# Prompt attention by pairs of heads side by side, each pair's output taken out first in VectorE's step

## The chip, the cores and the metric

One core of one Trainium2 chip. The metric is the device time of one execution of the whole kernel, in microseconds (us); the median of three runs of the kernel before is 2034.86 us (2034.53 to 2036.19).

## What is computed

One layer of a hybrid decoder, for a prompt of 1024 tokens and for 64 sample tokens: a token mixer (latent attention beside a depthwise convolution), cross attention to a memory, a gated feed-forward part. The change touches only the prompt's latent attention, 8 heads over 1024 positions with a causal mask:

```python
s = (jnp.einsum('bqhl,btl->bhqt', ql, c_keys) + jnp.einsum('bqhr,btr->bhqt', qp, pe_keys)) * ATTN_SCALE
s = jnp.where(pos[:, None] >= k_pos[None, :], s, NEG_INF)
pr = jax.nn.softmax(s, axis=-1)
o_lat = jnp.einsum('bhqt,btl->bqhl', pr, c_keys)
attn = jnp.einsum('bshl,lhv->bshv', o_lat, p['w_uv'])
```

The kernel forms keys (64 + 32 features per head) and values (64 per head) from the latents first, and multiplies `pr` by the values.

## The kernel before

The kernel is one program of stages, each with its own semaphores and with the instructions of every engine written out in order. `prompt_attention_stage` (L700) is the one in question. Its data are feature-major: `K.x[:, pair, token]` holds the attention output of heads 2·pair (partitions 0 to 63) and 2·pair+1 (64 to 127).

The work is cut into 64 **tiles** n = 8h + i: head h, block i of 128 queries. By causality block i sees keys 0 to 128(i+1)-1, so a tile of i = 7 has eight times the work of one of i = 0. For each tile:

- `scores(n)` on TensorE (L848): queries times keys into two of PSUM's banks (0, 1 or 2, 3 in turn).
- `find_top(n)` on VectorE (L1010, L1012, L1014): mask on the diagonal block, the row maximum, its negative.
- `exp(n)` on ScalarE (L941): probabilities into `prob[n % 2]`.
- `turn_tile(n)` on TensorE (L868): i+1 transposes of 128x128 into banks 4 and 5 (`turn`).
- `copy_turned(n)` on ScalarE (L949): to `prob_t[n % 2]`.
- `attend(n)` on TensorE (L878): i+1 products of turned probabilities (stationary, 128 columns) and `K.v[:, j, h, :]` (moving, 65 columns: 64 values and a column of ones, whose product is the row's sum). The result `o_acc` in bank 6 has a query per partition.
- `take_out(n)` on VectorE (L1020, L1024): the reciprocal of the sum, and the product with it into `o`.

An f32 matmul is two instructions in the profile, a transpose one. When a pair of heads is done, `o` of four blocks is transposed by `turn_pair` (L855) in two of the next pair's steps, and `copy_pair` (L955) puts it in `K.x`. Beside the tiles run the **jobs** that make queries (`q`, L826, three k-steps of 512 columns) and keys (`k`, L830, two); each has one accumulator bank and is read by ScalarE (L929, L932) and, for `q`, by three VectorE instructions of the rotary part (L999, L1000, L1003, `rope_job`). Four jobs stand at the start (`AT_START`), the others in steps i = 0, 1, 2 of each head. At given steps VectorE also does a part of the convolution's layer norm (`NORM_AT`, L1032, L1035), and ScalarE ends the stage with four Silu (L987).

The order is fixed by these loops; on TensorE:

```python
for n in range(TILES):
    turn_tile(n)
    if n + 2 < TILES:
        scores(n + 2)
    for what, which, half in jobs_beside(*divmod(n, QT)):
        job(what, which, half)
    if n >= 1:
        attend(n - 1)
```

VectorE's step n is `find_top(n + 2)`, `take_out(n - 1)`, the rotary part of the job. `attend(n)` waits until `take_out(n - 1)` has emptied `o_acc` (semaphore `o_out`).

## Time and profile before

| | |
|---|---|
| median of 3 runs | 2034.86 us (2034.53 to 2036.19) |
| the profiled execution | 2033.87 us, span 2032.0 us, mean granted clock 0.970 |
| TensorE matmul, of the span | 1857.1 us (91%) |
| VectorE, ScalarE, GpSimd | 1174.8, 481.8, 589.3 us |
| prompt attention, first to last tile's turn | 436.5 to 658.8 us |
| in it, busy: TensorE, VectorE, ScalarE | 209.8, 142.6, 100.9 of 222.3 us |

Times within the profile are from the start of the span. PE is TensorE's matmuls, PEld its weight loads (which overlap the matmuls), DVE is VectorE, ACT ScalarE. A matmul's duration contains its way through the array, which the next one overlaps; what one of a row of matmuls costs is the distance from start to start. In a merged row of N instructions it is (length - duration of one) / (N - 1). In forms such as `128*64 128x256` the first pair is rows*columns of the stationary operand, the second the moving operand.

### The profile page before, as it was taken

The page shows a single profiled execution, that of the slowest core. Times are in us where ns is not written, and L with a number is a line of the kernel's source. Part 1 is how long each engine was busy: PE and PEld are TensorE (multiplying, and loading weights), DVE is VectorE, ACT ScalarE, POOL GpSimd, SP SyncE. Part 2 cuts the span into 40 slices and gives each one's busy share as a digit, 9 for nine tenths or more (in the row PEclk, how much of TensorE's full clock was granted, in tenths as well). Part 3 has the DMA queues.
Part 4 walks back from the last instruction along what each step waited for, and adds up shares of the span by engine and source line. Part 5 has one row for each costly group of instructions (what it writes and reads, how often), then busy time and mean ns, then how long its engine had stood idle before and what let it go on. Part 6 is the DMA issues. An engine that isn't in the chain of part 4 may idle for free. (4 is left out here: it accounts for less than half of the span.)

```text
span 2032.0 us, 27594 instructions
## 1 busy us (share of the span) xinstructions
PE 1857.1 (91%) x10840; PEld 1657.8 (82%) x10840; DVE 1174.8 (58%) x1665; ACT 481.8 (24%) x810; POOL 589.3 (29%) x437
## 2 busy tenths in 40 slices
PE   6998888699999899899859989999999999999995
PEld 6998554356667898788729879999999999999983
DVE  7886599866665337333323797445454554545547
ACT  4021332144444423222222341001100100110011
POOL 3331489710000124321013722223222322232220
PEclk9999899799999999999989989999999999999997
DMA  5214422100000214400451211111111111111102
GB/s 160 99 42 58 173 94 94 32 31 1 1 1 1 85 48 156 144 21 10 164 213 52 94 42 42 42 41 41 51 42 41 41 51 42 41 41 49 44 14 88
DMA packets 42715, 128.42 MB, mean 63 GB/s; under 512 B 12464, under 2 KB 18736, under 8 KB 40016
## 3 DMA queue, kind: packets, MB, share of 16 engines
q1 hardware_dynamic: 39984, 105.17, 15.7%
q0 software_dynamic: 1792, 18.88, 2.4%
q10 hardware_dynamic: 864, 3.34, 0.5%
q8 instruction: 52, 0.85, 0.2%
q14 instruction: 23, 0.19, 0.0%
HBM read 118.81 MB, written 8.56 MB: 63 GB/s over the span
## 5 line engine op out<-in xcount | busy, mean ns | idle before, releaser
L252 POOL CAST w_hi<-raw 128x1024 fp32r<-128x1024 f32 x90 | 98.0, 1088 | 811.3 <-issue 319.7
L281 PE MATMUL ps<-xo_hi,w_hi 128*128 128x384 f32 (+1 forms) x1248 | 292.5, 332 | 18.3 <-DVE xo_lo L2644 6.2
L281 PE MATMUL ps<-xo_lo,w_hi 128*128 128x384 f32 (+1 forms) x1248 | 290.5, 331 | 0.0
L281 PE MATMUL ps<-xo_hi,w_lo 128*128 128x384 f32 (+1 forms) x1248 | 289.9, 330 | 0.0
L281 PEld LDWEIGHTS ps<-xo_hi,w_hi 128*128 128x128 f32 x1248 | 218.1, 189 | 22.2 <-issue 13.2
L254 POOL TENSOR_TENSOR w_lo<-raw,w_hi 128x1024 fp32r<-128x1024 f32 x90 | 221.1, 2456 | 7.2
L281 PEld LDWEIGHTS ps<-xo_lo,w_hi 128*128 128x128 f32 x1248 | 218.7, 190 | 0.2
L281 PEld LDWEIGHTS ps<-xo_hi,w_lo 128*128 128x128 f32 x1248 | 218.3, 189 | 0.0
L2597 DVE TENSOR_TENSOR xo<-ps,xo 128x768 f32<-128x768 f32 (+1 forms) x160 | 108.4, 719 | 130.6 <-PE ps L281 130.6
L377 DVE SCALAR_TENSOR_TENSOR x<-u_prompt,vecs,x 128x1024 f32<-128x1024 f32 x120 | 164.7, 1373 | 3.4
L2549 DVE TENSOR_TENSOR ffn_g_prompt<-ffn_g_prompt,ffn_rstd 128x1024 f32<-128x1024 f32 x22 | 67.4, 3062 | 167.2 <-ACT ffn_g_sample L2414 167.2
L281 PE MATMUL ps<-ffn_hid_hi,w_hi 128*128 128x384 f32 (+2 forms) x528 | 128.4, 342 | 4.8 <-DVE ffn_hid_lo L2586 4.8
L281 PE MATMUL ps<-ffn_hid_lo,w_hi 128*128 128x384 f32 (+2 forms) x528 | 123.6, 332 | 0.0
L281 PE MATMUL ps<-ffn_hid_hi,w_lo 128*128 128x384 f32 (+2 forms) x528 | 121.8, 329 | 0.0
L281 PE MATMUL ps<-hx_hi,w_hi 128*128 128x384 f32 (+1 forms) x384 | 90.9, 346 | 11.9 <-PEq L1475 5.4
L1540 POOL CAST w_hi<-raw 128x1024 fp32r<-128x1024 f32 x8 | 8.3, 1036 | 313.9 <-PE ps L281 283.1
L281 PEld LDWEIGHTS ps<-ffn_hid_hi,w_hi 128*128 128x128 f32 x528 | 91.1, 190 | 8.4 <-DVE ffn_hid_lo L2586 5.1
L878 PEld LDWEIGHTS ps<-v,mla_prob_t 128*128 128x128 f32 x576 | 72.8, 192 | 27.7 <-issue 23.4
L281 PEld LDWEIGHTS ps<-ffn_hid_lo,w_hi 128*128 128x128 f32 x528 | 91.9, 190 | 3.3 <-issue 3.0
L2423 ACT ACTIVATE ffn_hid_hi<-ffn_hid 128x1088 fp32r<-128x1088 f32 x22 | 24.5, 1114 | 289.5 <-PE ps L281 253.6
L281 PE MATMUL ps<-h_hi,w_hi 128*128 128x384 f32 x336 | 77.2, 338 | 16.7 <-POOL w_lo L473 11.7
L281 PEld LDWEIGHTS ps<-ffn_hid_hi,w_lo 128*128 128x128 f32 x528 | 91.6, 190 | 0.6
(348 smaller groups left out, 3352.6 us busy)
## 6 DMA issues: line engine op xcount, KB each, us to landing
raw<-in_units SPq DMA_DIRECT2D x128, 512.0 KB, 3.3
xs_keys<-in_cache_k_t SPq DMA_DIRECT2D x8, 1024.0 KB, 8.3
xs_vals<-in_cache_v_t SPq DMA_DIRECT2D x16, 512.0 KB, 13.3
x<-in_x_t SPq DMA_DIRECT2D x8, 544.0 KB, 9.3
out_y_t<-x SPq DMA_DIRECT2D x2, 1792.0 KB, 6.6
out_old<-in_x_t ACTq DMA_DIRECT2D x6, 544.0 KB, 4.0
mla_wq<-in_w_q_t SPq DMA_DIRECT2D x1, 1536.0 KB, 8.3
out_kv_latent_t<-c SPq DMA_DIRECT2D x1, 1088.0 KB, 13.0
```

Source lines behind the costliest of these rows:

```text
L252: nc.gpsimd.tensor_copy(K.w_hi[:, s, :], K.raw[:, s, :]).then_inc(K.hi_done[s], 1)
L254: nc.gpsimd.tensor_tensor(K.w_lo[:, s, :], K.raw[:, s, :], K.w_hi[:, s, :].bitcast(F32), ALU.subtract).then_inc(K.split_done[s], 1)
L281: mm = nc.tensor.matmul(out(at, n), w, x(k, at, n), start=first and k == 0 and p == 0, stop=last and k == len(tiles) - 1 and p == 2)
L377: ops.scalar_tensor_tensor(cv, u, scale, cv, ALU.mult, ALU.add).then_inc(tapped, 1)
L878: mm = nc.tensor.matmul(o_acc, prob_t[:, n % 2 * QT + j, :], K.v[:, j, h, :], start=j == 0, stop=j == i)
L1540: nc.gpsimd.tensor_copy(K.w_hi[:, s, :], K.raw[:, s, :]).then_inc(K.hi_done[s], 1)
L2423: nc.scalar.activation(hid_hi[:, slot, :], hid[:, :], ACT.Identity).then_inc(hid_hi_made, 1)
L2549: nc.vector.tensor_tensor(g_p, g_p, rstd[:, 0:SEQ], ALU.mult).then_inc(g_scaled, 1)
L2597: ins = nc.vector.tensor_tensor(y_at, acc, y_at, ALU.add)
```

## The change

Tiles are ordered by **rounds** of 16: `place(n)` takes the two heads of a pair in turn, block by block (tile 2m is head 2p, tile 2m+1 head 2p+1, same block i = m % 8). What was done per tile behind the turned copy is now done per pair m of tiles (32 pairs):

- `attend(m)`: the values are the stationary operand (64 columns) and the turned probabilities the moving one (128 columns). Head 2p's product goes to partitions 0 to 63 of `o_acc`, head 2p+1's to 64 to 127, the two in turn for each j. The result is feature-major.
- The sums come from `exp` (`accum_out` into `den`). `make_diagonals(m)` on VectorE takes the reciprocal (128x2) and makes two diagonal matrices of 128x128 from the identity; two f32 matmuls of ones and diagonal spread the inverses over partitions as `row_acc` (bank 6 too).
- `take_out(m)` on VectorE copies `row_acc` to `inv_row` and multiplies `o_acc` by it into `K.x`; it stands ahead of `find_top` in every odd step from 3. `o`, `turn_pair`, `copy_pair` and the column of ones are gone.
- `prob_t` has four buffers, `qh` four; the next pair's jobs (four q, two k) stand in steps r = 0 to 5 of a round, and `AT_START` has six jobs, of which three come behind the first two scores.

```diff
+        AT_START = [("q", 0, 0), ("k", 0, 0), ("q", 1, 0), ("q", 0, 1), ("k", 0, 1), ("q", 1, 1)]
+        FIRST_JOBS = 3
+        def place(n):
+            p, r = divmod(n, ROUND)
+            return 2 * p + r % 2, r // 2
+        def jobs_beside(n):
+            p, r = divmod(n, ROUND)
+            if p + 1 == HEADS // 2 or r >= 6:
+                return []
+            return [[("q", 2 * p + 2, 0), ("k", p + 1, 0), ("q", 2 * p + 3, 0), ("q", 2 * p + 2, 1), ("k", p + 1, 1),
+                     ("q", 2 * p + 3, 1)][r]]
...
+        o_acc, row_acc = K.ps[:, 6, 0:P], K.ps[:, 6, P:2 * P]
+        def half(h):
+            return slice(h % 2 * VH, (h % 2 + 1) * VH)
...
-            def attend(n):
-                h, i = divmod(n, QT)
-                pe.wait_ge(turned_copied, n + 1)
-                if n >= 1:
-                    pe.wait_ge(o_out, n)
+            def attend(m):
+                i = m % QT
+                pe.wait_ge(turned_copied, 2 * m + 2)
+                if m >= 1:
+                    pe.wait_ge(out, m)
                 for j in range(i + 1):
-                    mm = nc.tensor.matmul(o_acc, prob_t[:, n % 2 * QT + j, :], K.v[:, j, h, :], start=j == 0,
-                                          stop=j == i)
-                mm.then_inc(attended, 1)
+                    for n in (2 * m, 2 * m + 1):
+                        h = place(n)[0]
+                        nc.tensor.matmul(o_acc[half(h)], K.v[:, j, h, 0:VH], prob_t[:, n % 4 * QT + j, :], start=j == 0,
+                                         stop=j == i)
+                pe.wait_ge(diagonal_made, 2 * m + 2)
+                for par in range(2):
+                    nc.tensor.matmul(row_acc[half(par)], K.ones[:, 0:VH], diagonal[:, m % 2, par, :], start=True,
+                                     stop=True).then_inc(attended, 1)
...
+            for job_of in AT_START[:FIRST_JOBS]:
+                job(*job_of)
             scores(0)
             scores(1)
+            for job_of in AT_START[FIRST_JOBS:]:
+                job(*job_of)
...
-                if n >= 1:
-                    attend(n - 1)
+                if n % 2 == 0 and n >= 2:
+                    attend(n // 2 - 1)
...
-                nc.scalar.activation(prob[:, n % 2, 0:(i + 1) * P], score(n), ACT.Exp, bias=neg_top[:, i:i + 1],
-                                     scale=SCALE).then_inc(exped, 1)
+                nc.scalar.activation(prob[:, n % 2, 0:(i + 1) * P], score(n), ACT.Exp, bias=neg_top[:, r:r + 1],
+                                     scale=SCALE, accum_out=den[:, r:r + 1]).then_inc(exped, 1)
...
-            def take_out(n):
-                h, i = divmod(n, QT)
-                dve.wait_ge(attended, n + 1)
-                nc.vector.reciprocal(inv[:, i:i + 1], o_acc[:, VH:]).then_inc(inv_ready, 1)
-                dve.wait_ge(inv_ready, n + 1)
-                if h >= 2:
-                    dve.wait_ge(o_turned, 2 * (h // 2 - 1) + i // 4 + 1)
-                nc.vector.tensor_scalar(o[:, i, h % 2 * VH:(h % 2 + 1) * VH], o_acc[:, 0:VH], inv[:, i:i + 1], None,
-                                        ALU.mult).then_inc(o_out, 1)
+            def make_diagonals(m):
+                r = 2 * (m % QT)
+                dve.wait_ge(exped, 2 * m + 2)
+                nc.vector.reciprocal(inv[:, r:r + 2], den[:, r:r + 2]).then_inc(inv_ready, 1)
+                dve.wait_ge(inv_ready, m + 1)
+                for par in range(2):
+                    nc.vector.tensor_scalar(diagonal[:, m % 2, par, :], K.ident[:, :], inv[:, r + par:r + par + 1], None,
+                                            ALU.mult).then_inc(diagonal_made, 1)
+            def take_out(m):
+                p, i = divmod(m, QT)
+                dve.wait_ge(attended, 2 * m + 2)
+                if m >= 1:
+                    dve.wait_ge(out, m)
+                nc.vector.tensor_copy(inv_row[:, :], row_acc).then_inc(row_out, 1)
+                dve.wait_ge(row_out, m + 1)
+                nc.vector.tensor_tensor(K.x[:, p, i * P:(i + 1) * P], o_acc, inv_row[:, :], ALU.mult).then_inc(out, 1)
...
             for n in range(TILES):
+                if n % 2 == 1 and n >= 3:
+                    take_out(n // 2 - 1)
                 if n + 2 < TILES:
                     find_top(n + 2)
-                if n >= 1:
-                    take_out(n - 1)
-                for what, which, half in jobs_beside(*divmod(n, QT)):
+                if n % 2 == 1:
+                    make_diagonals(n // 2)
+                for what, which, half_of in jobs_beside(n):
                     if what == "q":
-                        rope_job(which, half)
+                        rope_job(which, half_of)
```

TensorE in the middle of a head, of before: every step has its turn (L868), scores (L848) and attend (L878).

```order
L878 MATMUL ps<-v,mla_prob_t 128x65 [waits mla_o_out,mla_turned_copied]
L878 MATMUL ps<-v,mla_prob_t 128x65 x3
L868 MATMUL ps<-ident,mla_prob 128x128 [waits mla_turned_copied,mla_exped]
L868 MATMUL ps<-ident,mla_prob 128x128 x5
L848 MATMUL ps<-mla_kh,mla_qh 128x512 [waits mla_exped]
L848 MATMUL ps<-mla_kh,mla_qh 128x512
L878 MATMUL ps<-v,mla_prob_t 128x65 [waits mla_o_out,mla_turned_copied]
L878 MATMUL ps<-v,mla_prob_t 128x65 x4
```

Here an attend stands between any two turns.

The same place of the change; 64x128 is the output's shape.

```order
L858 MATMUL ps<-ident,mla_prob 128x128 [waits mla_turned_copied,mla_exped]
L858 MATMUL ps<-ident,mla_prob 128x128 x4
L849 MATMUL ps<-mla_kh,mla_qh 128x512 [waits mla_exped]
L849 MATMUL ps<-mla_kh,mla_qh 128x256
L858 MATMUL ps<-ident,mla_prob 128x128 [waits mla_turned_copied,mla_exped]
L858 MATMUL ps<-ident,mla_prob 128x128 x5
L849 MATMUL ps<-mla_kh,mla_qh 128x512 [waits mla_exped]
L849 MATMUL ps<-mla_kh,mla_qh 128x384
L871 MATMUL ps<-mla_prob_t,v 64x128 [waits mla_out,mla_turned_copied]
L871 MATMUL ps<-mla_prob_t,v 64x128 x9
L875 MATMUL ps<-mla_diagonal,ones 64x128 [waits mla_diagonal_made]
L875 MATMUL ps<-mla_diagonal,ones 64x128
```

Two steps of turn and scores now stand between two attends, and each attend ends with two more matmuls that wait for VectorE's diagonals.

VectorE in the middle of a round, of the change:

```order
L1018 COPY mla_inv_row<-ps 128x128 [waits mla_out,mla_attended]
L1020 TENSOR_TENSOR x<-ps,mla_inv_row 128x128 [waits mla_row_out]
L997 TENSOR_TENSOR ps<-ps,causal 128x128 [waits mla_scored]
L999 TENSOR_REDUCE mla_top<-ps 128x1 [waits mla_masked]
L1001 TENSOR_SCALAR mla_neg_top<-mla_top 128x1 [waits mla_top_found]
L1007 RECIPROCAL mla_inv<-mla_den 128x2 [waits mla_exped]
L1010 TENSOR_SCALAR mla_diagonal<-ident,mla_inv 128x128 [waits mla_inv_ready]
L1010 TENSOR_SCALAR mla_diagonal<-ident,mla_inv 128x128
L997 TENSOR_TENSOR ps<-ps,causal 128x128 [waits mla_scored]
L999 TENSOR_REDUCE mla_top<-ps 128x1 [waits mla_masked]
L1001 TENSOR_SCALAR mla_neg_top<-mla_top 128x1 [waits mla_top_found]
```

An odd step has five instructions more than an even one; before, each step had its three of the maximum and two of taking out.

## Rows read from the trace of the kernel before

**Rows 1.** Stretches: us; busy (x instructions) PE, PEld, DVE, ACT, POOL; clock; DMA.
```profile
436.50:658.80 222.30, 209.79 (x1157) 147.20 (x1157) 142.61 (x366) 100.93 (x159) 0.00 (x0) 1.00 0.00 1
```

**Rows 2.** Groups of instructions, 436.5 to 658.8, costliest first.
```profile
L878 PE MATMUL ps<-v,mla_prob_t 128*128 128x65 f32 x549 | 69.5, 271 | 5.6 <-DVE mla_o L1024 5.6
L868 PE MATMUL ps<-ident,mla_prob 128*128 128x128 f32 x288 | 42.6, 275 | 3.1 <-ACT mla_prob L941 2.4
```

**Rows 3.** Who waited for whom, 436.5 to 658.8: total us, times, longest.
```profile
DVE ps L1010 <- PE ps L848: 26.5, 27, 2.0
PE ps L878 <- DVE mla_o L1024: 5.6, 17, 0.7
PE ps L830 <- DVE mla_part L1000: 5.6, 6, 1.0
```

**Rows 4.** TensorE's matmuls in order of time: start us, length, merged count, idle before.
```profile
580.47 1.06 PE L868 MATMUL ps<-ident,mla_prob 128*128 128x128 f32 x8
...
581.81 1.67 PE L878 MATMUL ps<-v,mla_prob_t 128*128 128x65 f32 x14
```

**Rows 5.** The same view: a query job of the stage, then the paged stage.
```profile
621.32 2.74 PE L826 MATMUL ps<-qn,mla_wq 128*128 128x512 f32 x6
...
376.56 1.89 PE L1246 MATMUL ps<-v,paged_q_lat 128*64 128x512 f32 x8
...
239.15 1.95 PE L1281 MATMUL ps<-x,paged_prob_t 128*64 128x256 f32 x16
```

**Rows 6.** The same view: the paged stage where the stationary operand's form changes.
```profile
230.14 0.40 PE L1254 MATMUL ps<-c,paged_q_lat 128*64 128x64 f32 x4
230.47 0.66 PE L1231 MATMUL ps<-ident,past_rope 128*128 128x128 f32 x4
...
373.09 1.89 PE L1246 MATMUL ps<-v,paged_q_lat 128*64 128x512 f32 x8
375.09 0.63 PE L1290 MATMUL ps<-paged_fold,paged_o 128*128 128x64 f32 x4
```

**Rows 7.** VectorE's groups of the whole span, shapes apart.
```profile
L1010 DVE TENSOR_TENSOR ps<-ps,causal 128x128 f32<-128x128 f32 x64 | 19.0, 296 | 27.0 <-PE ps L848 26.5
L1024 DVE TENSOR_SCALAR mla_o<-ps,mla_inv 128x64 f32<-128x64 f32 x64 | 18.2, 284 | 2.3
L1020 DVE RECIPROCAL mla_inv<-ps 128x1 f32<-128x1 f32 x64 | 10.4, 163 | 47.2 <-PE ps L878 47.0
L1012 DVE TENSOR_REDUCE mla_top<-ps 128x1 f32<-128x640 f32 x8 | 6.6, 824 | 0.3
...
L1012 DVE TENSOR_REDUCE mla_top<-ps 128x1 f32<-128x256 f32 x8 | 3.4, 425 | 0.3
L1982 DVE COPY xq_sample<-xp_q 128x128 f32 x3 | 0.7, 227 | 0.4
L1389 DVE TENSOR_TENSOR paged_fold<-ident 128x64 f32<-128x64 f32 x1 | 0.2, 160 | 0.0
```

**Rows 8.** ScalarE in order of time, and one of its groups (cross attention's exp).
```profile
581.57 1.02 ACT L949 ACTIVATE mla_prob_t<-ps 128x1024 f32<-128x1024 f32 x1 [0.99 <-PE ps L868]
...
L1915 ACT ACTIVATION_READ_ACCUMULATOR xp_prob<-ps,xp_neg_top 128x1 f32 x32 | 6.2, 192 | 0.0
```

**Rows 9.** The stage's start, engines mixed, in order of time.
```profile
433.24 0.68 DVE L1003 TENSOR_TENSOR mla_qh<-mla_part 32x512 f32<-32x512 f32 x1
...
436.55 0.30 PE L868 MATMUL ps<-ident,mla_prob 128*128 128x128 f32 x1 [2.40 <-ACT mla_prob L941]
```

**Rows 10.** The stage's end, engines mixed, in order of time.
```profile
658.78 1.02 ACT L949 ACTIVATE mla_prob_t<-ps 128x1024 f32<-128x1024 f32 x1 [1.25 <-PE ps L868]
...
660.92 1.97 PE L878 MATMUL ps<-v,mla_prob_t 128*128 128x65 f32 x16 [0.67 <-DVE mla_o L1024]
661.12 4.48 ACT L987 ACTIVATE x<-x,vecs 128x1088 f32<-128x1088 f32 x4
...
665.50 1.05 ACT L955 ACTIVATE x<-ps 128x512 f32<-128x512 f32 x2
```

More of the change, by code:

```diff
@@ L730, in prompt_attention_stage @@
         wq, wuk = sb("wq", [P, HEADS, KQ * P]), sb("wuk", [P, HEADS // 2, KC * P])
-        qh = [sb(f"qh{s}", [P, SEQ]) for s in range(2)]
+        qh = [sb(f"qh{s}", [P, SEQ]) for s in range(4)]
         kh = [K.kh] + [sb(f"kh{s}", [P, SEQ]) for s in range(1, 4)]
@@ L790, in _ @@
         def _(pool):
-            nc.gpsimd.memset(K.v[:, :, :, VH:], 1.0).then_inc(ones_set, 1)
             split_units(nc, pool, K, 1)
@@ L847, in scores @@
                     w = min(512, (i + 1) * P - at)
-                    mm = nc.tensor.matmul(score(n)[:, at:at + w], qh[h % 2][0:96, i * P:(i + 1) * P],
+                    mm = nc.tensor.matmul(score(n)[:, at:at + w], qh[h % 4][0:96, i * P:(i + 1) * P],
                                           key_buffer(h)[0:96, at:at + w], start=True, stop=True)
                 mm.then_inc(scored, 1)
-            def turn_pair(pair, half, to):
-                pe.wait_ge(o_out, (2 * pair + 1) * QT + 4 * half + 4)
-                for j in range(4):
-                    mm = nc.tensor.transpose(to[:, j * P:(j + 1) * P], o[:, 4 * half + j, :], K.ident[:, :])
-                return mm
             def turn_tile(n):
@@ L861, in turn_tile @@
                     pe.wait_ge(turned_copied, n)
-                    if pair_beside(n - 1) is not None:
-                        pair, half = pair_beside(n - 1)
-                        pe.wait_ge(out, 2 * pair + half + 1)
-                if pair_beside(n) is not None:
-                    turn_pair(*pair_beside(n), turned_pair(n)).then_inc(o_turned, 1)
-                for j in range(n % QT + 1):
+                for j in range(place(n)[1] + 1):
                     mm = nc.tensor.transpose(turn[:, j * P:(j + 1) * P], prob[:, n % 2, j * P:(j + 1) * P],
@@ L890, in _ @@
             pe.wait_ge(w_in, 32)
-            for what, which, half in AT_START:
-                job(what, which, half)
+            for job_of in AT_START[:FIRST_JOBS]:
+                job(*job_of)
             scores(0)
             scores(1)
+            for job_of in AT_START[FIRST_JOBS:]:
+                job(*job_of)
             pe.wait_ge(rooted, 2)
-            pe.wait_ge(ones_set, 1)
             for n in range(TILES):
@@ L901, in _ @@
                     scores(n + 2)
-                for what, which, half in jobs_beside(*divmod(n, QT)):
-                    job(what, which, half)
-                if n >= 1:
-                    attend(n - 1)
-            attend(TILES - 1)
-            pe.wait_ge(turned_copied, TILES)
-            for half in range(2):
-                turn_pair(HEADS // 2 - 1, half, turn[:, half * 512:(half + 1) * 512]).then_inc(o_turned, 1)
+                for job_of in jobs_beside(n):
+                    job(*job_of)
+                if n % 2 == 0 and n >= 2:
+                    attend(n // 2 - 1)
+            attend(TILES // 2 - 1)
         @block.scalar
@@ L971, in _ @@
                                      ).then_inc(rooted, 1)
-            for what, which, half in AT_START:
-                copy_job(what, which, half)
+            for job_of in AT_START[:FIRST_JOBS]:
+                copy_job(*job_of)
             exp(0)
             exp(1)
+            for job_of in AT_START[FIRST_JOBS:]:
+                copy_job(*job_of)
             for n in range(TILES):
                 copy_turned(n)
-                if pair_beside(n) is not None:
-                    copy_pair(*pair_beside(n), turned_pair(n))
                 if n + 2 < TILES:
                     exp(n + 2)
-                for what, which, half in jobs_beside(*divmod(n, QT)):
-                    copy_job(what, which, half)
+                for job_of in jobs_beside(n):
+                    copy_job(*job_of)
             for k in range(KU):
@@ L987, in _ @@
                 nc.scalar.activation(cv[k], cv[k], ACT.Silu, bias=vec(K, "b_cln", k)).then_inc(acted, 1)
-            for half in range(2):
-                copy_pair(HEADS // 2 - 1, half, turn[:, half * 512:(half + 1) * 512])
         @block.vector
@@ L1064, in _ @@
             for n in range(TILES):
+                if n % 2 == 1 and n >= 3:
+                    take_out(n // 2 - 1)
                 if n + 2 < TILES:
                     find_top(n + 2)
-                if n >= 1:
-                    take_out(n - 1)
-                for what, which, half in jobs_beside(*divmod(n, QT)):
+                if n % 2 == 1:
+                    make_diagonals(n // 2)
+                for what, which, half_of in jobs_beside(n):
                     if what == "q":
-                        rope_job(which, half)
+                        rope_job(which, half_of)
                 if n in NORM_AT:
```

66 lines of the change are left out of this document (25 added, 41 removed).

## Prediction

> **What bounds the kernel now.** I first read the stretches [rows 1]. From the first tile's turn (436.5) to the last one's (658.8) TensorE's matmuls are busy for 209.8 of 222.3 us at the full granted clock (1.00, the level of 2.4 GHz); VectorE has 142.6, ScalarE 100.9. So this stretch runs at TensorE's pace with short holes, and a change is worth what it takes from TensorE there. The groups [rows 2] show where it goes: the value products of L878 are the costliest, 69.5 us.
>
> What one instruction costs is read from start to start [rows 4]. Fourteen of L878 last 1.67 us: (1.67 - 0.27)/13 = 0.108 us each; with the start of a group 0.109. The transposes of L868 cost (1.06 - 0.275)/7 = 0.112. The moving operand of L878 is half as wide (65 against 128 columns) and yet it takes as long: what sets it is the stationary operand, 128 columns in both.
>
> The waits [rows 3] show the holes: 17 times L878 waits for VectorE to empty the accumulator (5.6 us), 6 times a key job for the rotary part (5.6 us). The end of the stage [rows 10] is ScalarE's: last turned copy from 658.78, four Silu from 661.12 to 665.6, then two more copies in 1.05 us; TensorE's last two attends lie under the Silu.
>
> **The value products.** 288 f32 products are 576 instructions before and after. What changes is the form: 64 stationary, 128 moving columns, the halves of the output in turn. The trace has this pattern in the paged stage [rows 5]. A 512-column instruction alone costs (2.74 - 0.59)/5 = 0.43 us. Eight of L1246, whose outputs alternate between partitions 0 to 63 and 64 to 127, last 1.89 us, which is four starts 0.43 apart: two run at once. Sixteen of L1281 with 256 columns last 1.95 us: (1.95 - 0.38)/7 = 0.224 per two, 0.112 each, where half of 0.43, 0.215, would be the price alone. So halves overlap, and 128 columns would go at 0.054 each. The other floor is the stationary load of 64 columns: L1254, with 64 moving columns that would need only 0.027, has (0.40 - 0.22)/3 = 0.060 [rows 6]. I take 0.060, the larger; the ends are 0.054 and, without overlap, 0.107.
>
> Up to the last turn 546 of 576 instructions lie before the change (tiles 62 and 63 come behind it), and 544 after it (pair 31 comes behind): 546 x 0.109 = 59.5, 544 x 0.060 = 32.6, together **-26.9 us**.
>
> **Inverses.** 31 pairs x 4 instructions of the same form (64 stationary, 128 moving): 124 x 0.060 = **+7.4**.
>
> **Changing the form.** TensorE now goes from 128 stationary columns to 64 and back in each of 31 pairs. Where the trace does this [rows 6], the last of L1254 starts at 230.14 + 0.40 - 0.22 = 230.32 and the first of L1231 at 230.47: 0.15 instead of 0.06, or 0.09 more. After L1246 the last pair starts at 374.39, streams until 374.82, and L1290 starts at 375.09: 0.27 (a wait for VectorE may be in it). I take 0.10, the nearer case, since nothing else is waited for there: 62 x 0.10 = **+6.2**; ends 0 and +16.7. The Trainium skill, "TensorEngine Tiling (Array Packing)", section Tiling Modes, says that changing the tiling mode, not just the tile, drains TensorE. A drain as long as what of a 0.27 us matmul remains behind its stream (0.16) would make this term +9.9; the rows lie on both sides of that.
>
> **Removed work and waits on TensorE.** 24 of the 32 pair transposes were in the loop: 24 x 0.109 = **-2.6**. The accumulator wait goes: 5.6 us of idle, and in each of the 17 cases the previous matmul's way through the array that stood bare (0.27 - 0.11 = 0.16): **-8.4**. Now `attend(m)` has two steps' turns and scores behind `attend(m-1)`, and `take_out(m-1)` has been put ahead of the maximum in VectorE's step, so it runs while TensorE does these.
>
> **New waits on TensorE.** In an odd step nothing stands between `scores` and the next turn. In the middle of a round the scores cover the copy (two instructions of 0.43 per 512 columns, so 0.214 a block and 1.7 for eight). At a round's end they do not: the turn of tile 16k waits for the copy of eight blocks, 0.2 + 1.02 us [rows 8], over scores of 0.2 us; before, `attend` of 14 instructions stood there (1.67 us, [rows 4]). Three such places, 1.0 each: **+3.0**. `attend` also ends in a wait for the diagonals, which follow `find_top` of the next tile; behind this wait stand the next turn and scores. From block 4 on I find that VectorE needs 0.30 + 0.82 + 0.15 [rows 7] (a negative costs about what a reciprocal of one column does) for the maximum and about 1.0 for the diagonals, against the turn, scores and attend (0.45 + 1.07 + 0.96) that TensorE has in between: just covered, 0.
>
> **The start.** Four jobs become six. The third, a query job, ends as before, and its rotary part at 433.9 [rows 9], then scores; the other three jobs start at 434.3. They wait for each other's readers (one bank): 2.6, then 1.6 of wait, 1.7, 1.5 of wait, 2.6 us: the first turn comes at about 444.3 instead of 436.55, +7.7. Two query jobs (2 x 6 x 0.429 = 5.1 us) leave the loop for it, and the 2.40 us hole before the first turn is filled by them: **+2.6**. The waits among jobs in the loop (5.6 us before) I leave as they are: 0. Five neighbouring pairs of jobs per round can wait, but behind an even step attend covers it, and in the first round there is little to cover with.
>
> **The last pair of heads** has no jobs. VectorE's load per pair of tiles: copy and multiply 0.28 + 0.30 (a copy of that size between SBUF tensors is 0.227, the mask's addition in PSUM 0.296; I put the copy out of PSUM between them), reciprocal 0.16, two diagonals. For these the nearest rows [rows 7] are 0.284 for 64 columns out of PSUM and 0.160 for 64 columns in SBUF; with 64 columns more at 0.07 that is 0.35 or 0.23, and I take 0.35. Together 1.45, with gaps 1.55, against 0.97 before. Two maxima of 256 columns are 2 x (0.30 + 0.43 + 0.15 + 0.10) = 1.95. So VectorE needs 3.5 us for block 1 of a pair and TensorE about 2.2. Blocks 0 to 2 together lose about 4 us, of which the old last head had about 1.5: **+2.5**.
>
> **ScalarE** gets a reading of the accumulator behind each exp, 64 x 0.192 = 12.3 us [rows 8], and loses eight copies of 0.5. It has 100.9 us of 222.3: covered, 0 (at a chain's bare places 0.19 each, inside the roundings above). VectorE gets 32 x 0.58 = 19 us: 162 of some 205; covered in the mean. GpSimd's memset goes: nothing waits for it.
>
> **The end.** From the last turn on ScalarE sets it: the two copies go, **-1.05**. TensorE's last attend (32 x 0.060 + 0.24) and VectorE's 0.6 lie under the Silu. TensorE then idles some 1 us longer before the next stage; I leave what follows from that at 0.
>
> **Sum:** -26.9 + 7.4 + 6.2 - 2.6 - 8.4 + 3.0 + 2.6 + 2.5 - 1.1 = **-17.3 us**. Against the profiled execution's 2033.87 that is 2016.6; the median of the runs is 1.0 above that execution, so 2017.5.
>
> **Rivals.**
> 1. *The halves do not overlap at 128 columns* (a load of one half keeps the other half's matmul from starting), so each costs 0.107: 544 x 0.047 + 124 x 0.047 = +31.4, or 2049, slower than before. The change is slower from 0.060 + 17.3/668 = 0.086 us each. For it: no row has this with 128 moving columns. Against: L1281 reaches its stream's pace with the same alternation. Chance 0.04.
> 2. *VectorE becomes the bound* also where there are jobs. In steps 0 to 5 of a round it has about 6.6 us of maxima, 8.4 of rotary parts, 4.7 for the pairs and up to 2.7 of layer norm or copies, some 20 to 22, against TensorE's 23. If its order costs another 1 us per four pairs it is +8: 2025.5. The Trainium skill, "TensorEngine Tiling (Array Packing)", section PSUM Bottleneck, says that tiling speeds up TensorE but not the emptying of PSUM, which may then bound. For it: VectorE's 162 of 205. Against: 26.5 us of its idle time before a maximum [rows 3] are waits for scores. Chance 0.15.
> 3. *The change of form is dear*, 0.27 each: +10.5, or 2028. Chance 0.08.
> 4. *It goes better*: 0.054 each (-4), no cost of form (-6): 2008. Chance 0.05.
>
> **How the numbers follow.** The forecast has 0.68, with a range of its own of +-5. From 2007 to 2028 the forecast and rivals 2 to 4 lie mostly inside; rival 1 and joint misses stay out. What differs by over 0.2% (4.1 us) can be told from no change. Faster: the forecast, 2 to 4 nearly whole, 0.88. Slower: rival 1 and a joint case of 2 and 3 with a further wait, 0.07. Same: 0.05.
>
> **What would show it.** Attends of 4(i+1) matmuls lasting 0.06 x count + 0.2 (32 in 2.1 us); no wait of the first for VectorE; first turn near 444, last near 642; the inverse's matmuls directly behind; a wait of about 1 us at the turn after a round's end. Wrong would be: starts of attend 0.1 us apart, TensorE waiting for `mla_diagonal` in most pairs, or maxima that VectorE starts without waiting for scores.

## The result, and the profile after

| | before | after |
|---|---|---|
| median of the runs of this comparison | 2037.86 us (2034.53 to 2039.43, 8) | 2028.18 us (2025.59 to 2035.19, 8) |
| ratio to the runs of before | | 0.996, interval 0.9949 to 0.9972 |
| profiled execution, its span | 2033.87, 2032.0 us | 2025.59, 2023.6 us |
| stage: start of the first job to start of the last tile's turn | 233.0 us | 228.0 us |
| stage: first job to the next stage's first ScalarE instruction | 242.2 us | 236.2 us |
| in it: first turn to last turn | 221.1 us | 208.1 us |

The change makes the kernel faster, by 0.4% (0.28 to 0.51%), where 0.85% was forecast: about half. The time lies 0.2 us above the forecast's range; the kernel before, too, came out 3.0 us above the 2034.86 us from which the forecast started. Below, "the stage" is the time from the first query job's first matmul to the next stage's first ScalarE instruction: the total moves by several us from one execution to the next, but the same kernel run again (below) gave 236.9 us here against 236.2. One execution of `again` (2360.02 us) and one of `no_inverse` (6324.25 us) were far slower than all others; the ratios and profiles leave them out.

The stretch from the first turn to the last, after (columns as in [rows 1]):

```profile
444.00:652.20 208.20, 188.32 (x1234) 113.72 (x1233) 151.07 (x400) 101.43 (x212) 0.00 (x0) 0.98 0.00 1
```

TensorE is busy for 188.3 of 208.2 us, where [rows 1] have 209.8 of 222.3. So 21.5 us of its work are gone, but the idle time has grown from 12.5 to 19.9 us, and the clock is no longer full throughout (0.98).

The groups of this stretch and its borders, after (as [rows 2] and [rows 7]), TensorE, VectorE, ScalarE:

```profile
L858 PE MATMUL ps<-ident,mla_prob 128*128 128x128 f32 x288 | 44.2, 281 | 14.4 <-ACT mla_prob_t L943 14.2
...
L871 PE MATMUL ps<-mla_prob_t,v 128*64 128x128 f32 x576 | 38.5, 278 | 1.1 <-ACT mla_prob_t L943 1.1
...
L875 PE MATMUL ps<-mla_diagonal,ones 128*64 128x128 f32 x128 | 12.6, 275 | 0.2 <-DVE mla_diagonal L1010 0.2
```
```profile
L997 DVE TENSOR_TENSOR ps<-ps,causal 128x128 f32<-128x128 f32 x62 | 18.4, 297 | 32.4 <-PE ps L849 32.0
L1010 DVE TENSOR_SCALAR mla_diagonal<-ident,mla_inv 128x128 f32<-128x128 f32 x64 | 15.4, 284 | 1.1
...
L1020 DVE TENSOR_TENSOR x<-ps,mla_inv_row 128x128 f32<-128x128 f32 x32 | 9.3, 291 | 1.1
L1018 DVE COPY mla_inv_row<-ps 128x128 f32<-128x128 f32 x32 | 9.2, 287 | 7.6 <-PE ps L875 7.5
```
```profile
L935 ACT ACTIVATION_READ_ACCUMULATOR mla_prob<-ps,mla_neg_top 128x1 f32 x62 | 12.0, 193 | 0.0
```

The value products, 69.5 us in [rows 2], are now 38.5, with 12.6 for the inverses. The first group names the loss: the turn, which waited 3.1 us in all, now waits 14.4, for ScalarE's copy of the tile turned before it. VectorE still waits 32 us for scores before its maxima, so in the mean it isn't the bound.

Who waited for whom, TensorE, 436 to 665, after (as [rows 3]):

```profile
PE ps L858 <- ACT mla_prob_t L943: 14.2, 13, 2.3
...
PE ps L831 <- DVE mla_part L987: 4.6, 5, 1.8
PE ps L827 <- ACT mla_kh L926: 2.6, 4, 1.3
PE ps L871 <- ACT mla_prob_t L943: 1.1, 1, 1.1
PE ps L827 <- DVE mla_part L987: 1.0, 1, 1.0
PE ps L875 <- DVE mla_diagonal L1010: 0.2, 1, 0.2
```

The 5.6 us for the accumulator are gone, and the diagonals cost 0.2 us in the whole stage. The waits of jobs are 8.2 us, of which 2.9 (1.58 and 1.28) lie before the first turn and had been forecast there as 3.1; the 5.3 behind it match the 5.6 of before. What is new are the 13 waits for a copy.

**The products and the inverses**, TensorE in order of time, after:

```profile
456.93 0.44 PE L871 MATMUL ps<-mla_prob_t,v 128*64 128x128 f32 x4
...
457.20 0.39 PE L875 MATMUL ps<-mla_diagonal,ones 128*64 128x128 f32 x4
457.52 0.44 PE L858 MATMUL ps<-ident,mla_prob 128*128 128x128 f32 x2
```

No diagonals are waited for, and the four matmuls of the inverses with the way back to 128 columns take 457.52 - 457.20 = 0.32 us (forecast 0.24 + 0.10).

**The first round's end**, engines mixed, after. Tile 14 and tile 15 are the last two of the round, 16 the first of the next:

```profile
496.18 2.55 DVE L1027 RECIPROCAL mla_ln_rstd<-mla_ln_rstd 128x384 f32<-128x384 f32 x1
...
496.82 1.01 ACT L943 ACTIVATE mla_prob_t<-ps 128x1024 f32<-128x1024 f32 x1
...
497.97 1.06 PE L858 MATMUL ps<-ident,mla_prob 128*128 128x128 f32 x8 [1.21 <-ACT mla_prob_t L943]
...
499.28 0.15 DVE L1001 TENSOR_SCALAR mla_neg_top<-mla_top 128x1 f32<-128x1 f32 x1
499.35 2.14 DVE L1027 RECIPROCAL mla_ln_rstd<-mla_ln_rstd 128x320 f32<-128x320 f32 x1
499.47 0.37 ACT L935 ACTIVATE mla_prob<-ps,mla_neg_top 128x128 f32<-128x128 f32 x1 [1.64 <-DVE mla_neg_top L1001]
...
499.82 1.01 ACT L943 ACTIVATE mla_prob_t<-ps 128x1024 f32<-128x1024 f32 x1
...
500.98 0.44 PE L858 MATMUL ps<-ident,mla_prob 128*128 128x128 f32 x1 [1.72 <-ACT mla_prob_t L943]
...
502.08 5.05 PE L827 MATMUL ps<-qn,mla_wq 128*128 128x512 f32 x6
...
507.05 1.97 PE L871 MATMUL ps<-mla_prob_t,v 128*64 128x128 f32 x32
```

The second wait, 1.72 us, is the forecast's wait behind a round's end (in the other rounds 0.98 and 0.98). The first, 1.21, stands at the turn of tile 15 and was not forecast. During the second the granted clock falls to its level of 1.2 GHz, from 499.9 to 506.7, 6.8 us: the six matmuls of a query job need 5.05 us instead of 2.74 [rows 5]. In the kernel before the clock was full from first to last turn. Thirty-two products last 1.97 us: (1.97 - 0.28)/31 = 0.055 each.

**The last tile**, engines mixed, after, and the stage's end behind it:

```profile
648.79 1.75 PE L871 MATMUL ps<-mla_prob_t,v 128*64 128x128 f32 x28
...
649.69 0.16 DVE L1007 RECIPROCAL mla_inv<-mla_den 128x2 f32<-128x2 f32 x1
649.81 1.11 ACT L935 ACTIVATE mla_prob<-ps,mla_neg_top 128x1024 f32<-128x1024 f32 x1 [2.31 <-DVE mla_neg_top L1001]
...
650.91 1.01 ACT L943 ACTIVATE mla_prob_t<-ps 128x1024 f32<-128x1024 f32 x1
...
652.07 1.06 PE L858 MATMUL ps<-ident,mla_prob 128*128 128x128 f32 x8 [1.21 <-ACT mla_prob_t L943]
653.17 1.02 ACT L943 ACTIVATE mla_prob_t<-ps 128x1024 f32<-128x1024 f32 x1 [1.25 <-PE ps L858]
...
655.51 4.48 ACT L976 ACTIVATE x<-x,vecs 128x1088 f32<-128x1088 f32 x4
```

This is the mechanism bare. Tile 62 has been turned by 648.9, but ScalarE copies it only at 650.91: `exp` of tile 63 is written ahead of the copy and waits 2.31 us for VectorE's maximum. The turn of tile 63 needs the turned banks empty and so waits for that copy. An attend stands between the two turns here (28 products from 648.79), but it is not long enough. The same place in the kernel before, TensorE in order of time:

```profile
653.63 1.23 PE L878 MATMUL ps<-v,mla_prob_t 128*128 128x65 f32 x10
654.69 0.93 PE L868 MATMUL ps<-ident,mla_prob 128*128 128x128 f32 x7
656.12 1.52 PE L878 MATMUL ps<-v,mla_prob_t 128*128 128x65 f32 x12 [0.49 <-DVE mla_o L1024]
657.68 1.07 PE L868 MATMUL ps<-ident,mla_prob 128*128 128x128 f32 x8
```

The chain from a tile's scores over maximum, `exp` and the copy of the tile before it to that tile's turn was there before: it took 3.9 us (653.8 to 657.68) and takes 4.1 now (648.0 to 652.07). What covered it were two attends and a wait for the accumulator, just enough. Now there is one attend in two steps, and each of its products costs half. In an odd step nothing but the scores is left between two turns, and in an even one, as here, the attend can still be too short.

**Block 4 of the first round**, the same view, after:

```profile
471.13 0.68 DVE L990 TENSOR_TENSOR mla_qh<-mla_part 32x512 f32<-32x512 f32 x1
471.74 0.68 DVE L1074 COPY mla_kh<-kh 32x1024 f32<-32x1024 f32 x1
...
472.45 0.30 DVE L997 TENSOR_TENSOR ps<-ps,causal 128x128 f32<-128x128 f32 x1
...
473.82 0.79 ACT L935 ACTIVATE mla_prob<-ps,mla_neg_top 128x640 f32<-128x640 f32 x1 [3.06 <-DVE mla_neg_top L1001]
...
474.61 0.59 ACT L943 ACTIVATE mla_prob_t<-ps 128x512 f32<-128x512 f32 x1
...
475.34 0.74 PE L858 MATMUL ps<-ident,mla_prob 128*128 128x128 f32 x5 [1.47 <-ACT mla_prob_t L943]
```

The same again, behind an odd step without an attend, the first after the six steps with jobs. VectorE comes late to the maximum of this block: it is at a rotary part and a copy of keys until 472.4. The 13 waits are: 1.47, 2.26, 0.87 at block 4 of rounds one to three; 1.21, 1.09, 1.09, 1.21 at the odd head's last block of each round; 1.72, 0.98, 0.98 behind a round's end; 0.60, 0.44, 0.24 in the last pair.

### The profile page after: what moved, and what is told of

Read it like the earlier page. It is cut to its first block and busy times, and to the rows that moved or that the text cites. A ratio compares the mean times of both kernels' runs of the same rounds, so it can differ in the third digit from the quotient of the medians.

```text
span 2023.6 us, 27819 instructions
## 1 busy us (share of the span) xinstructions
PE 1841.5 (91%) x10936; PEld 1626.3 (80%) x10936; DVE 1188.6 (59%) x1697; ACT 482.5 (24%) x866; POOL 590.2 (29%) x436
## 5 line engine op out<-in xcount | busy, mean ns | idle before, releaser
L281 PE MATMUL ps<-xo_hi,w_hi 128*128 128x384 f32 (+1 forms) x1248 | 291.8, 332 | 17.5 <-DVE xo_lo L2643 5.4
L254 POOL TENSOR_TENSOR w_lo<-raw,w_hi 128x1024 fp32r<-128x1024 f32 x90 | 221.1, 2456 | 7.2
L281 PE MATMUL ps<-hx_lo,w_hi 128*128 128x384 f32 (+1 forms) x384 | 86.1, 333 | 0.0
```

The source lines that it names most:

```text
L254: nc.gpsimd.tensor_tensor(K.w_lo[:, s, :], K.raw[:, s, :], K.w_hi[:, s, :].bitcast(F32), ALU.subtract).then_inc(K.split_done[s], 1)
L281: mm = nc.tensor.matmul(out(at, n), w, x(k, at, n), start=first and k == 0 and p == 0, stop=last and k == len(tiles) - 1 and p == 2)
```

## The experiments

Theory H (holes): what the form of the products gave, the new order takes back, since in odd steps nothing stands between scores and the next turn while the copy stands behind an `exp` that waits for the maximum. Rivals: O, that the halves' overlap is worth less than thought; V, that VectorE's added work bounds (rival 2). All times of the stage are from profiled executions. `again` to `apart` were run together (before: 2038.39, median of 26 runs), `no_inverse` to `odd_all` too (before: 2037.17, 11 runs), the last two too (2036.19, 12 runs).

| kernel | median, us | ratio (interval) | stage, us | first to last turn, us | turn's waits for a copy: us, times | half clock between first job and last turn, us |
|---|---|---|---|---|---|---|
| after | 2028.18 | 0.996 (0.9949 to 0.9972) | 236.2 | 208.1 | 14.2, 13 | 6.8 |
| again | 2032.62 | 0.9973 (0.9958 to 0.9988) | 236.9 | 208.1 | 14.2, 13 | 8.2 |
| norm_late | 2028.0 | 0.9943 (0.9921 to 0.9965) | 235.2 | 205.3 | 12.7, 15 | 6.8 |
| swap | 2029.59 | 0.9954 (0.9939 to 0.997) | 235.2 | 205.3 | 10.6, 9 | 10.2 |
| apart | 2038.65 | 1.0002 (0.9987 to 1.0016) | 244.6 | 216.5 | 8.7, 9 | 0 |
| no_inverse | 2029.04 | 0.9951 (0.9933 to 0.997) | 233.4 | 203.6 | 16.2, 17 | 6.8 |
| odd | 2017.65 | 0.991 (0.9893 to 0.9928) | 222.4 | 203.5 | 10.3, 13 | 6.8 |
| odd_norm | 2012.05 | 0.9885 (0.9864 to 0.9905) | 219.0 | 200.1 | 9.1, 13 | 3.4 |
| odd_all | 2009.44 | 0.9871 (0.9848 to 0.9894) | 218.5 | 199.5 | 7.9, 12 | 3.4 |
| all_apart | 2028.91 | 0.9958 (0.9939 to 0.9976) | 236.0 | 217.0 | 7.2, 9 | 6.8 |
| all_q5 | 2008.18 | 0.9859 (0.9838 to 0.988) | 215.6 | 196.6 | 3.7, 11 | 6.8 |

The half clock must be taken into account where two kernels are compared. Some of it falls on the jobs ahead of the first turn, where the kernels' code is the same: in `norm_late` and `swap` the fourth job lasts 4.44 us there instead of 2.74, so 3.4 us of half clock cost 1.7 (in `no_inverse` 4.28, and its neighbour is slowed too). In the last five kernels it stands near the first turn: from there to the next turn that waits for a copy the same instructions take 11.7 us with 6.8 us of half clock (`odd`, `all_apart`, `all_q5`) and 10.4 with 3.4 (`odd_norm`, `odd_all`), 1.3 us less. "At the same clock" below means with these prices taken off; it is an estimate from these rows.

### again: the change unaltered

> The changed kernel once more, beside the others of this set. If the changed kernel's own holes (theory) explain the forecast's miss, the profile has again about 14 us of waits of TensorE's turns for ScalarE's copy, first turn near 444, last near 652, and a stretch of half clock after the first round's end. If the miss was chance of that one execution (rival), the last turn comes near 642. Time 2025 to 2030 us.

The stage takes 236.9 us against 236.2, with the same waits to a tenth and the same 6.8 us of half clock at the same place. The 0.7 us are its first job, which a further 1.4 us of half clock lengthen from 2.74 to 3.42; first to last turn take 208.1 us in both. So differences of the stage of over 1 us mean something once the clock is taken off; the total moved more than that with the clock in other stages (the medians are 4.4 us apart, the intervals of the ratios overlap).

### norm_late: the layer norm's parts in other steps

```diff
-            NORM_AT = {n: j for j, n in enumerate((12, 13, 14, 20, 21, 22, 28))}
+            NORM_AT = {n: j for j, n in enumerate((8, 10, 12, 24, 26, 28, 40))}
```

> Only NORM_AT is changed: the seven parts of the layer norm go to steps 8, 10, 12, 24, 26, 28, 40, even steps in the middle of a round, from 12, 13, 14, 20, 21, 22, 28. Theory: VectorE's queue at the first round's end (three reciprocals of 2.5 us) and behind the second round's jobs makes holes that let the clock fall for some 7 us and cost waits of 1.7 and 2.3 us; without them the loop is shorter by about 3 (half clock) + 0.7 + 1.4, some 5 us, and the clock stays 1.00 in the loop: 2021 to 2023 us against 2026 to 2028. Rival (the layer norm lies in VectorE's free time, the clock falls anyway): no difference, within 1 us.

The reciprocals no longer stand at the first round's end. The waits there (1.21 and 1.72) become 1.09 and 0.98, and block 4's of round two falls from 2.26 to 0.87, but 0.61 and 0.20 appear at blocks 5 and 6 of round one. Half clock is as long as in after, 3.4 us of it now ahead of the first turn; the forecast for this run was that it goes. The stage is 1.0 us shorter, where 5 were expected. The layer norm makes these places worse and is not the cause: what is left at these places is what the rounds without any layer norm have (1.09, 0.98 and 0.87).

### swap: ScalarE copies the turned tile ahead of exp

```diff
             for n in range(TILES):
-                copy_turned(n)
+                ahead = place(n)[1] >= FIRST_SWAPPED and n % 2 == 1 and n + 2 < TILES
+                if not (n > 0 and place(n - 1)[1] >= FIRST_SWAPPED and n % 2 == 0):
+                    copy_turned(n)
+                if ahead:
+                    copy_turned(n + 1)
```

(`FIRST_SWAPPED = 3`.)

> Only ScalarE's order is changed: from block 3 of a round on, in odd steps the copy of the next turned tile stands ahead of the exp that follows it, not behind. Theory: at a round's end the copy, whose data lie ready, waits behind an exp that waits for VectorE; four such places cost 1.1 to 1.2 us, in the last round 0.2 more; swapped, they go: 4 to 6 us less, 2021 to 2024 us. Rival (the wait is for the exp itself, or for VectorE, and moves): within 1 us, or up to 2 slower in the middle of the rounds, where the exp is then late.

The last tile's turn now waits 0.21 us, for its own exp, instead of 1.21 for the copy; the four waits at the odd head's last block are gone, which shows that the order on ScalarE made them. But at the first round's end one wait of 2.70 us takes the place of two, since VectorE is at a reciprocal of the layer norm (503.92 to 506.4) when the next maximum could start. The stage gains 1.0 us, and has 3.4 us more of half clock, so 2.7 at the same clock, where 4 to 6 were expected. The order on ScalarE is a part of it, and a small one alone: where nothing is left for TensorE to do, the next wait stands close behind.

### apart: the halves no longer in turn

```diff
-                for j in range(i + 1):
-                    for n in (2 * m, 2 * m + 1):
+                for n in (2 * m, 2 * m + 1):
+                    for j in range(i + 1):
```

> Only the order of attend's matmuls is changed: all blocks of the lower half, then all of the upper half, so that neighbours write the same half. Theory (two halves run at once): each of the matmuls costs its stream, 0.107 us, instead of 0.055; 544 x 0.052 = 28 us more in the loop, perhaps 3 less where it fills holes: 2050 to 2056 us. Rival (the gain comes from the stationary load of 64 instead of 128 columns, at 0.06 us each): no difference.

The stage grows by 8.4 us and the whole gain is gone (ratio 1.0002), where 25 to 28 us more had been expected. TensorE in order of time, of apart:

```profile
555.75 2.56 PE L871 MATMUL ps<-mla_prob_t,v 128*64 128x128 f32 x25
558.05 0.32 PE L875 MATMUL ps<-mla_diagonal,ones 128*64 128x128 f32 x1
558.15 0.27 PE L871 MATMUL ps<-mla_prob_t,v 128*64 128x128 f32 x1
...
558.80 1.08 PE L858 MATMUL ps<-ident,mla_prob 128*128 128x128 f32 x8
```

Four instructions more per pair cost 0.44 us here (runs of 17, 21, 25 and 29 last 1.69, 2.13, 2.56 and 3.00), 0.109 each against 0.055 in turn. From its first product to the next turn an attend with its inverses takes 0.27, 0.49, 0.71, 0.93, 1.15 and 1.36 us longer than in after at blocks 2 to 7, and no longer at blocks 0 and 1, where the halves still overlap around the seam (last section): 18.3 us up to the last turn, where 28 were expected. The stage shows less. The half clock, worth 2.8 us in after (next section), is gone, so it is 11.2 us at the same clock; and the waits for copies fell by 5.5 us and from 13 to 9, each with 0.16 us of its own beside it. So some 6 us of what the products lost lay in the holes. The stage alone, with its small price, speaks for O as much as for H; all_apart tries it with the holes filled.

### no_inverse: without the normalisation

```diff
-                pe.wait_ge(diagonal_made, 2 * m + 2)
-                for par in range(2):
-                    nc.tensor.matmul(row_acc[half(par)], K.ones[:, 0:VH], diagonal[:, m % 2, par, :], start=True,
-                                     stop=True).then_inc(attended, 1)
...
-                nc.vector.tensor_copy(inv_row[:, :], row_acc).then_inc(row_out, 1)
-                dve.wait_ge(row_out, m + 1)
-                nc.vector.tensor_tensor(K.x[:, p, i * P:(i + 1) * P], o_acc, inv_row[:, :], ALU.mult).then_inc(out, 1)
+                nc.vector.tensor_copy(K.x[:, p, i * P:(i + 1) * P], o_acc).then_inc(out, 1)
...
-                if n % 2 == 1:
-                    make_diagonals(n // 2)
```

It leaves out the division by the row's sum: the diagonals, their matmuls and the product with the inverses.

> The changed kernel without its normalisation: the two diagonals, their matmuls and the multiply by the inverses are left out, and the output block is copied as it is (one VectorE instruction per pair instead of five). It prices the inverses: by the trace 0.22 us of TensorE per pair (7 us in the loop) and 1.2 us of VectorE per pair. If TensorE's sum decides: 5 to 8 us less. If VectorE's load is what makes the holes (rival): clearly more than 8 us less, and the 14 us of waits for the copy shrink too. If the order of the steps makes them (theory), at most 3 of the 14 us go.

VectorE loses four of the five instructions that the pair added, TensorE four of 0.055 us per pair (6.8 us in all). The stage gains 2.8 us (half clock is as long as in after), less than TensorE's own share, and the waits for copies rise to 16.2 us. So V falls for the load that the pairs added: with VectorE relieved of it the holes remain, and they give back nothing; they even take some of what TensorE has less to do. That VectorE is late in single steps, by rotary parts or the layer norm, is another matter, see block 4, norm_late and all_q5.

### odd: the jobs in odd steps

```diff
-        AT_START = [("q", 0, 0), ("k", 0, 0), ("q", 1, 0), ("q", 0, 1), ("k", 0, 1), ("q", 1, 1)]
+        AT_START = [("q", 0, 0), ("k", 0, 0), ("q", 1, 0)]
...
+            if n == 0:
+                return [("q", 0, 1)]
+            if r in (1, 3):
+                return [("k", p, 1) if r == 1 else ("q", 2 * p + 1, 1)]
+            if p + 1 < HEADS // 2 and r in (7, 9, 13, 15):
+                return [{7: ("q", 2 * p + 2, 0), 9: ("k", p + 1, 0), 13: ("q", 2 * p + 3, 0),
+                         15: ("q", 2 * p + 2, 1)}[r]]
+            return []
```

> Only the places of the jobs are changed. The start keeps three (q and k of head 0, q of head 1); the other three stand in steps 0, 1, 3. In later rounds the next pair's four stand in steps 7, 9, 13, 15 and its last two in steps 1 and 3 of its own round: odd steps, which have no attend behind their scores. The layer norm stays where it was. Theory (the forecast's gain is lost in holes where an odd step has nothing to cover a copy or an exp with, and in jobs that wait for each other's readers): the waits for ScalarE's copy fall from 14 us to 4 or 5, the job waits of the start and first round from 6 us to 2, and the clock stays 1.00 in the loop (3 us): from the first job to the last turn 14 to 18 us less than the changed kernel's 228, total 2012 to 2017 us. Rival (VectorE's sum of work sets the pace, 0.58 us more per pair than before): the holes move elsewhere and less than 4 us is won.

The stage falls from 236.2 to 222.4 us and the total to 2017.65, the forecast's own number, which is chance. A job is 1.7 to 2.6 us of TensorE's work, and in an odd step it stands where no attend does. The waits of jobs for the rotary part and the key copies fall from 8.2 to 1.0 us, since two jobs are no longer neighbours; those for copies from 14.2 to 10.3. The half clock at the round's end is gone, but one as long stands near the first turn, so the 13.8 us are not the clock's.

### odd_norm and odd_all

To odd, odd_norm adds the layer norm in even steps (first diff); odd_all also copies one turned tile ahead of exp, in step 13 of each round:

```diff
-            NORM_AT = {n: j for j, n in enumerate((12, 13, 14, 20, 21, 22, 28))}
+            NORM_AT = {n: j for j, n in enumerate((10, 26, 42, 44, 52, 56, 58))}
...
-                copy_turned(n)
+                ahead = n % ROUND == ROUND - 3
+                if not (n % ROUND == ROUND - 2):
+                    copy_turned(n)
+                if ahead:
+                    copy_turned(n + 1)
```

> As the run before, and the layer norm's seven parts go to steps 10, 26, 42, 44, 52, 56, 58, one reciprocal a round. Theory of holes: the reciprocals in steps 12 to 14 still delay three maxima; spread, 1 to 2 us less than the run before. Rival of VectorE's sum: no difference.

> As the run before, and in step 13 of each round ScalarE copies the next turned tile ahead of the exp of step 15's tile. It meets only the last round's end, where no job stands: 1.0 to 1.2 us less than the run before if that copy is what the turn waits for; nothing if the job had covered it.

The stage: 222.4, 219.0, 218.5 us. The layer norm is worth 3.4 here, of which 1.3 are the clock's, so 2.1 at the same clock (expected 1 to 2; norm_late gave 1.0). The swap on ScalarE gives 0.5: it takes the last turn's wait of 1.22 us, as expected, and the time from the turn of 613.2 to the last one falls by 1.0, but each of the three full rounds, where a job covered the copy, grows by some 0.15 (51.40 to 51.56 from the wait at block 3 of round one to that of round two). Waits of TensorE in the stage, of odd_all:

```profile
PE ps L862 <- ACT mla_prob_t L947: 7.9, 12, 1.4
...
PE ps L875 <- ACT mla_prob_t L947: 1.1, 1, 1.1
PE ps L835 <- DVE mla_part L995: 1.0, 1, 1.0
PE ps L862 <- ACT mla_prob L939: 0.2, 1, 0.2
```

Four of 1.40 are left, one per round, at block 3's first turn:

```profile
453.79 0.63 PE L862 MATMUL ps<-ident,mla_prob 128*128 128x128 f32 x4 [1.40 <-ACT mla_prob_t L947]
```

### all_apart: odd_all with the halves not in turn

The edit of apart, in odd_all.

> The order of odd_all (no wait of any size is left in a round), with a pair's attend matmuls in the order of apart: all of the lower half's first, then all of the upper half's. It tells whether the small price of apart (6 us of the median) was the worth of the overlap or only what the holes let through. Theory (the halves' overlap is worth 5 us a round of TensorE's work, and holes absorbed most of it in apart): with the holes gone the stage from the first job to the next stage lasts 235 to 238 us against 218.5 in odd_all, +17 to +19 us, so 2025 to 2029. Rival (the overlap is worth little in truth, the array's queue runs ahead either way): +4 to +8 us, 2013 to 2018, with TensorE's wait for the copied tiles again above 12 us.

The stage is 236.0 us, 17.5 more than odd_all, within the 17 to 19 expected; 1.3 of it are the clock's, so 16.2 at the same clock, where apart had 11.2 of the 18.3 that its rows show. The waits for copies hardly change (7.9 to 7.2). So O falls, of which 4 to 8 us were expected: the halves' overlap is worth some 16 us of the stage once few holes cover it. Edit and instructions are the same in both, and only the order around them differs.

### all_q5: one query job from step 3 to step 5

```diff
-            if r in (1, 3):
+            if r in (1, 5):
```

> odd_all with one query job of each round moved from step 3 to step 5, past which its rotary part is moved on VectorE too. In odd_all one wait for a copied tile of 1.40 us stands at block 3's turn in each round, right behind that job's rotary part. Theory (the rotary part delays that step's maximum and so the copy): the four waits of 1.40 go from block 3, and come back at block 5 or 6 no larger than 0.7 where the steps are longer, 2 to 4 us less, 2005 to 2008. Rival (steps 3 and 5 have the same slack, the wait only moves): 2009 to 2010, four waits of about 1.4 at a later block.

The stage falls by 2.9 us to 215.6 (by 4.2 at the same clock, as much as the waits), and the four waits of 1.40 are gone; one of 0.89 is the largest left. TensorE, of all_q5:

```profile
PE ps L862 <- ACT mla_prob_t L947: 3.7, 11, 0.9
```

So the rotary part behind that job had delayed the next maximum. The medians (2009.44 and 2008.18) can't tell the two apart, the stage can. all_q5 is the fastest version tried: 1.4% (1.2 to 1.62%) less than before, where the change as it was made has 0.4%.

## Why the prediction was half right

To the last turn the forecast's terms say -16.2 us (without the stage's end); measured from the first job: -5.0. Term by term:

- **Value products, -26.9 at 0.060 each.** Right, and better: 0.055 (24, 28, 32 of them last 1.53, 1.75, 1.97 us). 544 x 0.005 = 2.7 us more gain. The neighbour with 256 columns [rows 5] was the right row, and the floor of 0.060 taken from [rows 6] was not one. Rival 1 is out.
- **Inverses and change of form, +13.6.** Right. Per pair 0.32 us from the first matmul of the inverses to the next turn, and 0.09 for the way in (the six matmuls of the job before start at 454.16 and last 2.84, so the last starts 0.59 before their end, at 456.41, and streams for 0.43; the products start at 456.93): 0.41 against 0.44, so 0.9 us better. The wait for the diagonals is 0.2 us in all, as argued. The Trainium skill ("TensorEngine Tiling (Array Packing)", section Tiling Modes) says that a change of mode drains TensorE; here such a change costs about 0.1 us each way; rival 3 is out, and rival 4 was right on the products only.
- **Accumulator waits, -8.4, and pair transposes, -2.6.** Right: the wait list has no wait for `out`.
- **The start, first turn near 444.3.** 443.99, in a stage that began 0.6 us earlier, so 0.3 late. The waits of jobs behind it, left as they were, are 5.3 us against 5.6. Right, but luck had a part: they are neighbours at other places, and `odd` shows that they could have gone.
- **"In the middle of a round the scores cover the copy."** This is the step that failed. It counted the copy from the end of its turn. ScalarE's order was not followed: the copy stands behind the exp of the next tile, and that behind a maximum which starts only when the next scores end. Three such places of 1.0 us were counted, behind the rounds' ends, and 2.5 us for the last pair: 5.5. The trace has 13 waits of 14.2 us and 0.2 for diagonals, +8.9. The three places counted were 1.72, 0.98 and 0.98, as worked out; the ones that were missed are block 4 of three rounds (4.6 us), behind an odd step of which the forecast said that its scores cover the copy, and the odd head's last block of each round (4.6 us), where the scores are those of block 0 or there are none, and an attend of 28 products is too short a cover.
- **What a wait costs beyond itself.** By the prediction's own price (0.27 - 0.11) each also lays bare 0.16 us of the previous matmul's way through the array. That was counted for the waits that went and not for those that came: 13 x 0.16 = +2.1.
- **The clock.** Not thought of: 6.8 us at half of it, worth 2.3 us in one query job (5.05 against 2.74) and 0.5 in two scores (1.06 against 0.60): +2.8. What brought it down is open (last section).
- **The end, -1.05.** 9.16 us from last turn to the next stage before, 8.20 after: -0.96.

The balance: -16.2 - 2.7 - 0.9 + 8.9 + 2.1 + 2.8 = -6.0 against -5.0 measured; 1.0 us stays unexplained. Outside the stage the profiled executions differ by 2.3 us in favour of after, within what one kernel differs from itself.

Rival 2 came out near the time (2025.5), and in part by luck. It saw that VectorE's order could cost 8 us, but took its load for the cause. The trace has VectorE idle for 32 us before maxima, and no_inverse took most of the new load away and left the holes. In one place it was right: right behind the steps with jobs, at block 4, VectorE is late by its rotary part, and all_q5 shows that moving such a part takes waits away. These are 4.6 of the 14.2 us. The Trainium skill's warning that emptying PSUM may bound ("TensorEngine Tiling (Array Packing)", section PSUM Bottleneck) points to the right chain: what is waited for is a copy out of PSUM. But its place in ScalarE's order counts for more than its duration (1.02 us): with the copy ahead of exp (swap) the last turn waits 0.21 us instead of 1.21.

The range was a little narrow for the same reason: its upper end of 2028 came from a price of the form, and the waits, the one term of the sum that rested on an argument instead of a row, had no range of their own.

## What to carry to other kernels

When work is taken out of every step of a pipeline and put in every second one, follow each engine's written order through one step that has lost its filler or keeps a shorter one, waits of the other engines included, and price what the bottleneck's engine waits for there; a cover in the mean is none in the step. Then move the work that can stand anywhere (here the jobs) into the steps that have become empty. And judge a part of a change by undoing it where there are few holes, and at the same clock: the same edit cost 8.4 us of the stage in the kernel with holes and 17.5 in the one without, 11.2 and 16.2 at the same clock.

## What the runs showed of the hardware

- **The two column halves run ahead of each other, a little.** In apart an inverse on the lower half, written behind all products, starts at 558.05, ahead of three products on the upper half that stand before it in the program (the first at 558.15). So halves overlap even at the seam between two rows of products: the average price in apart, (3.00 - 0.28)/28 = 0.097 us, is below the marginal one of 0.109.
- **The clock fell near short waits, and not by a rule that these waits show.** In both executions of the change that were profiled it fell about 0.6 us into the wait of 1.72 us, with one of 1.21 and 1.3 us of turn and scores before it (497.97 to 499.26), and stayed at 1.2 GHz for 6.8 us. In norm_late it fell within the pair of waits of 1.09 and 0.98 at the first round's end, for 3.4 us, and not at the same pair at the ends of the next two rounds (561.84 and 616.17). In swap it fell 1.3 us after the wait of 2.25 at block 4, in after not at the one of 2.26. Apart had waits of 1.71 and 1.99 and stayed at 2.4 GHz. So what brought it down stays open.
- **Two diagonals take less than twice one.** The two instructions of L1010 last 0.48 us together where one has 0.284, so 0.09 of it overlaps.
- **Reading the accumulator behind an exp** takes 0.193 us, 64 times, as cross attention's did [rows 8]. It lies in each chain from maximum to copy; no run had it alone.
